# Sums of squares of queries and keys: two rounded products in place of one fp32 product, and a later place for the keys' sums

## The reference, cut to what matters

```python
def rms_norm(x, g):
    x32 = x.astype(jnp.float32)
    y = x32 * lax.rsqrt(jnp.mean(x32 * x32, axis=-1, keepdims=True) + EPS)
    return (y * g.astype(jnp.float32)).astype(x.dtype)

def split_kv(kv, k_g):
    b, n, _ = kv.shape
    k = rms_norm(kv[..., :QK_WIDTH].reshape(b, n, H_DIFF, 2, DH), k_g)   # DH = 64
    v = kv[..., QK_WIDTH:].reshape(b, n, H_DIFF, DV)
    return k, v
...
            kc, vc = split_kv(hc @ w_in[:, K0:G0], even_k_norm[e])   # 256 context tokens
            proj = h @ w_in                                          # 1024 tokens
            q, k, v = split_qkv(proj, even_q_norm[e], even_k_norm[e])
```

## Time and profile before

| | |
|---|---|
| time, median of 3 runs | 2914.75 us (2913.84 to 2916.66) |
| profiled execution | 2915.26 us, of which the span is 2913.2 us |
| TensorE busy | 2833.8 us (97%) |
| VectorE busy | 1432.3 us (49%) |
| ScalarE busy | 913.7 us (31%) |
| GpSimd busy | 627.4 us (22%), 316 instructions |

### The profile page before, as it was taken

One profiled execution on the slowest core, in us unless ns is written; L12 is line 12 of the kernel. 1 busy time (PEld: TensorE's weight loads), 2 busy tenths in 40 slices (PEclk: granted clock), 3 DMA queues, 4 the chain that ended last, 5 costly groups with the idle time before them and its releaser, 6 DMA issues.

```text
span 2913.2 us, 34625 instructions
## 1 busy us (share of the span) xinstructions
PE 2833.8 (97%) x14282; PEld 2355.5 (81%) x14282; DVE 1432.3 (49%) x1522; ACT 913.7 (31%) x1084; POOL 627.4 (22%) x316
## 2 busy tenths in 40 slices
PE   7999999999999999999999999999999999999997
PEld 4878778887788888788888888888877888888886
DVE  6478128877422226545555565555766213131236
ACT  4332227763211113444442222222333112121122
POOL 0111115104122214222221111111032221222222
PEclk9999999999999999999999999999999999999999
DMA  7211440023111112111111111111021111111113
GB/s 227 69 29 39 150 145 1 1 75 93 50 45 51 51 44 87 51 45 50 44 54 37 37 34 32 37 37 37 23 80 53 49 51 44 51 51 51 44 55 112
DMA packets 276868, 168.51 MB, mean 58 GB/s; under 512 B 5617, under 2 KB 270193, under 8 KB 276337
## 3 DMA queue, kind: packets, MB, share of 16 engines
q1 hardware_dynamic: 275280, 162.88, 18.9%
q10 hardware_dynamic: 1440, 3.51, 0.3%
HBM read 162.17 MB, written 4.19 MB: 57 GB/s over the span
## 4 chain that ended last, share of the span: by engine, by line
issue 52%; PE 36%; POOL 7%; DVE 3%; ACT 1%; DVEq 1%; POOLq 0%; ACTq 0%
PE PS L1472 10%; PE PS L1474 10%; PE PS L1473 10%; POOL Wlo L403 7%; ACT exp L667 1%; DVE acol L1155 1%; PE PS L1644 1%; PE PS L1781 1%; PE PS L1565 1%; PE PS L1653 0%; PE PS L1634 0%; DVE acol L1152 0%; DVE exp L1173 0%; DVEq L1156 0%; PE PS L1664 0%
## 5 line engine op out<-in xcount | busy, mean ns | idle before, releaser
L403 POOL TENSOR_TENSOR Wlo<-Wraw,Whi 128x1024 fp32r<-128x1024 f32 (+1 forms) x240 | 572.1, 2384 | 2141.3 <-ACT Whi L465 2141.3
L1472 PE MATMUL PS<-Bh,Whi 128*128 128x512 f32 x2176 | 859.7, 395 | 4.9 <-POOL Wlo L403 3.6
L1474 PE MATMUL PS<-Bh,Wlo 128*128 128x512 f32 x2176 | 848.8, 390 | 0.0
L1473 PE MATMUL PS<-Bl,Whi 128*128 128x512 f32 x2176 | 848.4, 390 | 0.0
L465 ACT ACTIVATE Whi<-Wraw 128x1024 fp32r<-128x1024 f32 (+1 forms) x240 | 250.4, 1043 | 781.1 <-PE PS L1474 778.7
L1472 PEld LDWEIGHTS PS<-Bh,Whi 128*128 128x128 f32 x2176 | 409.7, 188 | 94.2 <-POOL Wlo L403 6.6
L1474 PEld LDWEIGHTS PS<-Bh,Wlo 128*128 128x128 f32 x2176 | 409.3, 188 | 86.3
L1473 PEld LDWEIGHTS PS<-Bl,Whi 128*128 128x128 f32 x2176 | 409.8, 188 | 83.5 <-issue 1.2
L1472 PE MATMUL PS<-Hh,Whi 128*128 128x512 f32 x1120 | 444.8, 397 | 6.6 <-POOL Wlo L403 3.6
L1474 PE MATMUL PS<-Hh,Wlo 128*128 128x512 f32 x1120 | 437.4, 391 | 0.0
L1473 PE MATMUL PS<-Hl,Whi 128*128 128x512 f32 x1056 | 412.4, 391 | 0.0
(11 more groups left out here) (323 smaller groups left out, 3060.0 us busy)
## 6 DMA issues: line engine op xcount, KB each, us to landing
Wraw<-in_w_in SPq DMA_DIRECT2D x64, 512.0 KB, 4.0
Wraw<-in_w_down SPq DMA_DIRECT2D x38, 512.0 KB, 3.8
adaV<-in_ada_w SPq DMA_DIRECT2D x16, 1024.0 KB, 5.1
Wraw<-in_odd_w_in SPq DMA_DIRECT2D x32, 512.0 KB, 4.1
Wraw<-in_w_up SPq DMA_DIRECT2D x32, 512.0 KB, 4.1
Wraw<-in_even_w_in SPq DMA_DIRECT2D x24, 512.0 KB, 3.8
adaW<-in_ada_w SPq DMA_DIRECT2D x8, 1024.0 KB, 11.3
Wraw<-in_even_w_out SPq DMA_DIRECT2D x14, 512.0 KB, 3.8
```

What stands on the lines that cost most here:

```text
L403: pool.tensor_tensor(Wlo[:, slot, 0:tiles, :], Wraw[:, slot, 0:tiles, :], Whi[:, slot, 0:tiles, :].bitcast(F32), ALU.subtract).then_inc(lo ...
L1472: mm(out, Whi[:, u % 2, k, :], hi[:, k, c], start=(k == 0), stop=False)
L1473: mm(out, Whi[:, u % 2, k, :], lo[:, k, c], start=False, stop=False)
L1474: return mm(out, Wlo[:, u % 2, k, :], hi[:, k, c], start=False, stop=(k == KT - 1))
```

## The change: the sums

For sets 2 to 7 ScalarE squares twice: once into `qsq` (fp32) as before and once into `qsh` (rounded to fp32r). GpSimd subtracts, `qsl = qsq - qsh`, and signals `qsl_ready`. TensorE multiplies `qsh` and `qsl` one after the other by `blocksr`, a rounded copy of `blocks`, and accumulates both. Sets 0 and 1 stay as they were. The sums of sets 4 to 7 move from between the two halves of a unit to the middle of its second half, 12 products later.

```diff
@@ pool_program
-        splits(0, BASE["eo"])
+        def squares_low(c):
+
+            n = N if c < 4 else NK
+            pool.wait_ge(sem("qsq_ready"), c + 1)
+            pool.tensor_tensor(qsl[:, 0:n], qsq[:, 0:n], qsh[:, 0:n].bitcast(F32), ALU.subtract).then_inc(sem("qsl_ready"), 1)
+
+        pool.wait_ge(sem("const_loaded"), 16)
+        pool.tensor_copy(blocksr[:, :], blocks)
+        splits(0, BASE["q"] + 4)
+        for c in range(2, 8):
+            squares_low(c)
+            split(BASE["q"] + c + 2, c % 2)
+        split(BASE["q"] + 10, 0)
+        split(BASE["q"] + 11, 1)
+        splits(BASE["g"], BASE["eo"])
@@ act_program, qk_square
-            act.activation(qsq[:, 0:N], acc(u % 2), SQUARE)
-            if c >= 4:
-                act.activation(qsq[:, N:NK], bank(6, NC), SQUARE)
+            if c == 2:
+                act.wait_ge(sem("fourier_psum"), GROUPS)
+            for sq in (qsq, qsh) if c >= 2 else (qsq,):
+                act.activation(sq[:, 0:N], acc(u % 2), SQUARE)
+                if c >= 4:
+                    act.activation(sq[:, N:NK], bank(6, NC), SQUARE)
             act.drain().then_inc(sem("qsq_ready"), 1)
@@ pe_program, qk_sum
-            for h in range(2):
-                ins = mm(bank(4 + h), blocks, qsq[:, h * 512:(h + 1) * 512], start=True, stop=True)
-            if c >= 4:
-                ins = mm(bank(7, NC), blocks, qsq[:, N:NK], start=True, stop=True)
+            outs = [(bank(4), slice(0, 512)), (bank(5), slice(512, N))] + ([(bank(7, NC), slice(N, NK))] if c >= 4 else [])
+            if c >= 2:
+                pe.wait_ge(sem("qsl_ready"), c - 1)
+            for out, t in outs:
+                if c < 2:
+                    ins = mm(out, blocks, qsq[:, t], start=True, stop=True)
+                else:
+                    mm(out, blocksr[:, :], qsh[:, t], start=True, stop=False)
+                    ins = mm(out, blocksr[:, :], qsl[:, t], start=False, stop=True)
             ins.then_inc(sem("qssq"), 1)
@@ pe_program, the keys' and values' units
-            qk_sum(c + 3)
-            half(BASE["k"] + c, 1)
+            if c == 0:
+                qk_sum(c + 3)
+            half(BASE["k"] + c, 1, mid=(lambda: qk_sum(c + 3)) if c else None)
...
-            if c == 0:
-                qk_sum(7)
-            else:
+            if c:
...
-            half(BASE["v"] + c, 1)
+            half(BASE["v"] + c, 1, mid=None if c else lambda: qk_sum(7))
```

More of the change, by code:

```diff
@@ L194, in build @@
     qR = at("qR", s0 + 5 * KB, [NK])
+    qsh = at("qsh", x0 + 36 * KB, [NK], F32R)
+    qsl = at("qsl", x0 + 41 * KB, [NK], F32R)
+    blocksr = at("blocksr", x0 + 67 * KB, [P], F32R)
     rope = at("rope", y0 + 16 * KB, [2, N])
```

## The result

| | before | after |
|---|---|---|
| time, median of 22 runs each, side by side | 2914.87 us (2913.54 to 2916.66) | 2919.38 us (2916.89 to 2921.8) |
| span of the profiled execution | 2913.2 us | 2917.5 us |
| VectorE busy | 1432.3 us | 1444.5 us |
| GpSimd busy | 627.4 us | 648.4 us |

The ratio is 1.0015 [1.0009, 1.0021]: the changed kernel is 4.5 us slower, less than the 0.2% named in the prediction. The forecast was 2917.4 us, +2.6, with a range of 2916 to 2920.5.

The account below looks back on a forecast made before the run. TensorE was taken to set the pace, VectorE close behind and bounding from set 4; 5.5 us saved in the sums against about 8 us of claim waits gives +2.55, forecast 2917.4 us, range 2916 to 2920.5.

Parts of the forecast that it names:

- holds unsure by 0.3 us: Range of the forecast: VectorE's blocks of 2.0 us unsure by 0.3, six times, beside the runs' spread of 1.5 us.
- The sums: On TensorE, each query sum 0.80 us shorter and each key sum 0.98 us shorter, 5.5 us in all.
- GpSimd holds VectorE, and where: GpSimd's subtractions hold VectorE's two-SBUF-input instructions about 2 us; key sets 17.25 us apart, unit 13 starting at 272.0.
- Rival A: No VectorE instruction is held, the clock stays and 5.5 us are gained: 2909.3 us; chance 0.08.
- Rival C: VectorE held twice a set in three key sets, the squares' subtraction following the weights': +10.6, 2925.4 us; chance 0.04.
- The waits at claims: TensorE waits at the claims of units 10 to 13, some 1, 2.3, 2.3 and 2.3 us, about 8 us.
- A fall of the clock in waits of 2.3 us is left out: TensorE's clock priced at no loss, since 2.49 us idle between 440 and 450 us left it at 1.00.
- So the 2.55 us stay: After unit 13 nothing of VectorE is near, so the stage's +2.55 us reaches the kernel's end.
- Rival B: At 180.00 us VectorE's product starts before GpSimd's subtraction, so GpSimd waits: -4.5, 2910.3 us; chance 0.12.
- The distance of 0.25 us: In set 1 GpSimd starts near 179.75, 0.25 us before VectorE wants its product at 180.00.

Follow-up runs that it names:

- e1: The changed kernel without GpSimd's subtraction of the squares, the second product of each sum taking the rounded squares again; 2910.66 us, 0.9983 of the kernel before.
- e2: The changed kernel with the keys' sums back between the two halves of a unit; 2918.91 us, 1.0014 of the kernel before.
- e6: The changed kernel with 16 unused products over 256 columns on TensorE before the claim of unit 13; 2918.64 us, 1.001 of the kernel before.
- e8: The changed kernel with the new sums for sets 2 and 3 only, keys' sums fp32 in their old places; 2918.56 us, 1.0008 of the kernel before.
- e5: The kernel before with only the keys' sums moved to the middle of the second half; 2915.4 us, 1.0002 of the kernel before.
- e7: The changed kernel with set 2 keeping its fp32 sum and sets 3 to 7 in the new form; 2910.83 us, 0.9985 of the kernel before.
- e3: The changed kernel with GpSimd's first subtraction of squares also waiting until VectorE has finished with set 1's root; 2912.23 us, 0.9992 of the kernel before.
- e4: The kernel before with second squares and the subtraction added but unused, fp32 sums in their old places; 2915.27 us, 1.0004 of the kernel before.

## Why the prediction was right or wrong

The time, 2919.38 us, lies within the forecast's range, 2916 to 2920.5, but the kernel moved by 4.5 us and not by 2.6. The mechanism is as predicted; the size came within the range in part by luck, since the range was drawn for holds unsure by 0.3 us and for the spread of the runs, and what filled it was the clock.

**The sums** (-5.5 us): right. 5.7 us in the stage of the kernel after, 5.5 left in e1.

**GpSimd holds VectorE, and where:** right, set by set. The product of set 1, one rotary product of set 2 and the final sums of sets 1, 3, 4, 5 and 6 took 3.2 to 3.4 us. VectorE's period was 17.3 us (17.25 predicted), ScalarE's roots waited for VectorE, unit 13 started at 272.94, or 272.1 without the 0.81 us from before the stage (272.0 predicted). Rival A falls. One small wait isn't in the prediction's sum: by its own times unit 8's weights end at 189.4, about when unit 7 does; they ended at 190.17 and unit 8 started 0.2 us late. Rival C didn't occur: the squares' subtraction never took the port a second time ahead of a final sum.

**The waits at claims** (1, 2.3, 2.3, 2.3 us): 0.93, 2.04, 0.49 and 2.07 us, plus 0.27 us each that isn't listed, which makes the long ones 2.3. The third is short only because the clock's fall in unit 11 had used up 1.6 us: VectorE sets the pace there, so that fall cost nothing.

**The step that failed** inside the forecast is this one: "A fall of the clock in waits of 2.3 us is left out". I took one stretch with 2.49 us of idle time at a clock of 1.00 for a rule. Behind unit 13, where nothing of VectorE is near any more, the fall costs its full 1.6 us: the stage should have been +2.55 and was +4.37. Where no fall came in the last unit, in e2, e6 and e8, the stage was +2.81, +2.87 and +2.75 us. That is the forecast's term, some 0.25 us above it; that the lower clock itself is what makes unit 13 longer is read from its products, 0.42 us apart.

**"So the 2.55 us stay":** nothing is given back close behind the stage (the profiled kernel after is 5.2 us late at 302 us and at 422 us), but elsewhere the clock falls in some executions and not in others. Followed along GpSimd's weight subtractions, the profiled kernel after is 0.8 us late ahead of the stage, 5.2 behind it, 5.3 at 707 us and 4.4 from 748 us to the end. In between, from 724 to 736 us, the mean clock was 0.86 in the kernel before and 1.00 in the kernel after. The other traces agree: e2 to e5, also at 1.00, gain 0.8 us there; e1, e6, e7 and e8, at 0.86 to 0.93, don't. And in e1, e2, e3 and e7 the clock fell at a wait of the attention near 440 us (mean 0.57 over 4 us in e1 and e3), and 1.8 to 2.1 us were lost between 422 and 661 us. So in their profiled executions a part of e1's, e3's and e7's stage gain of 4.0 to 5.5 us is gone again; their medians show 2.7 to 4.3 us. One profile of each kernel can't say how often an execution has which fall; that stays open, and with it the split of the last 2 us of the 4.5.

**Rival B:** its mechanism and its price were right (-4.5 worked out, -4.03 in e3 and -4.38 in e7), and it truly hung on who is first at 180 us. The distance of 0.25 us was read off the trace of before, and it held: 0.28 us in the kernel after and again in e2, e4, e6 and e8.

**e4** shows a limit of the account. I expected the late VectorE to cost TensorE 3 us with the old sums too. It cost 0.7, all at unit 8, where VectorE held GpSimd, and nothing at units 11 to 13. How much of a late engine reaches the path depends on how late it is against the cover behind the sum: with the same cover, e8, whose VectorE is 3 to 5 us later, paid 1.1 us a unit.

## What to carry to other kernels

Before adding a GpSimd instruction with SBUF operands, lay its start over VectorE's instructions with two SBUF inputs, and do it again for the sets after, since the delay moves every later meeting; a pattern can lock in and stay after its cause is gone (e8). If two instructions meet within some tenths of a microsecond, build both orders: one added wait, or one instruction dropped, was worth over 8 us in this stage, 1.6 us of them the clock. And price a new TensorE wait of about 2 us with the clock behind it: none or 1.6 us, unless something else hides it.

## What the runs showed of the hardware

- A waiting GpSimd subtraction takes the port in the 0.07 to 0.08 us between two VectorE instructions, with great regularity: in sets 3 to 6 of the kernel after the final sum took 3.21 to 3.25 us every time. A VectorE shuffle (e3, 1.37 us) and a reciprocal (e7, 8.15 us) beside a subtraction had their usual length, and so had the subtraction.
- A wait of TensorE of nearly the same length can go either way. Waits of 2.04 and 2.07 us in the kernel after were followed by a granted clock of 0.61 and 0.60 over 4 us. In e2 one of 2.07 us (to 238.04) was followed by 1.00, and the next, 2.08 us (to 255.33), by 0.60 from 256 to 260; three waits of 1.1 us in e8 by 1.00. The same wait of 2.49 us for `exp` in the attention left 1.00 in the kernel before and 0.57 in e3:

```profile
444.52 0.48 PE L1781 MATMUL PS<-kT,qT 64*128 64x256 f32 x1 [2.49 <-ACT exp L667]
```

```profile
444.00:448.00 4.00, 3.48 (x22) 2.38 (x23) 3.54 (x7) 2.71 (x5) 3.86 (x2) 1.00 0.00 0
```

```profile
440.62 0.79 PE L1807 MATMUL PS<-kT,qT 64*128 64x256 f32 x1 [2.49 <-ACT exp L689]
```

```profile
440.00:444.00 4.00, 3.38 (x9) 1.86 (x11) 2.27 (x3) 2.63 (x4) 3.86 (x2) 0.57 0.00 0
```

The first two lines are of the kernel before, the last two of e3: the first product behind the wait is 0.48 us long in the one and 0.79 us in the other. The Trainium skill (TensorE: Matmul & The Clock Gate, section "What's actually happening") says that the gate's watch runs freely and isn't reset by the kernel. That fits equal waits with different outcomes; the runs here don't show the watch itself.
